# PEER gates by accumulating indirect DMAs into a table in device memory, in place of one-hot products on TensorE

## The chip, the core and the metric

The kernel runs on one core of one Trainium2 chip. The metric is the device time of one execution, in microseconds (us). The three timed executions of the kernel before took 2057.8, 2057.73 and 2062.33 us; their median is 2057.8 us. The engines are called by their names in the profile: PE is TensorE (PEld is its weight load), DVE is VectorE, ACT is ScalarE, POOL is GpSimd, and SP is SyncE, which here only issues DMAs.

## The reference, cut to what matters

One layer: a token mixer (projection with `w_in`, eight heads of stick-breaking attention, eight of retention, projection with `w_out`), a layer norm, the PEER block below, and a layer norm. There are 256 tokens of width 2048 and 16384 experts. Every token picks 16 experts for each of 8 heads; the pick's softmax weight is its gate:

```python
cand = (s_top[:, :, 0, :, None] + s_top[:, :, 1, None, :]).reshape(n_tok, PEER_HEADS, 256)
cand_idx = (i_top[:, :, 0, :, None] * PEER_KEYS + i_top[:, :, 1, None, :]).reshape(n_tok, PEER_HEADS, 256)
best, pos = lax.top_k(cand, PEER_TOPK)
expert_idx = jnp.take_along_axis(cand_idx, pos, axis=-1)
gate = jax.nn.softmax(best, axis=-1)
...
act = jax.nn.gelu(jnp.einsum('thkd,td->thk', u, xb), approximate=False)   # u = expert_u[idx]
return jnp.einsum('thk,thkd->td', g_b * act, v)                          # v = expert_v[idx]
```

## The kernel before, in words

The kernel gathers no expert rows. It computes the activation of every expert for every token, multiplies each by the sum of the gates that the token gave to that expert (zero where the token did not pick it), and multiplies the result with the whole of `expert_v`. The activations stand in SBUF in `wexp`: partition = expert within a tile, then `NT` = 128 tiles, then 256 tokens. Matrices are multiplied in float32r as three products of a high and a low part, so each piece of weights that SP loads into `raw` is split by ACT (`split_hi`) and by DVE or POOL (`split_lo`), and PE waits for both.

The stages in order of time:

- The projection with `w_in`: 14 column groups (`dense`), 16 k-tiles each. SP loads a group as 8 DMAs of 512 KB into the four slots of `raw`, and waits before each until the slot has been split (L279). The attention and retention heads are worked in between the k-tiles of groups 4 to 13. Then the projection with `w_out`, the layer norm and the query projection follow.
- The score stage: `PAIRS` = 64 pairs of expert tiles. Per pair, SP loads 2 MB of `expert_u` (L310), DVE transposes it (`turn_u`, L1393), ACT and POOL or DVE split it, PE multiplies it with the tokens (L640, L655), ACT and DVE bring the result out (`second_half_out`, `add_halves`), and ACT applies the gelu. In pairs 0 to 25 (`PAIRS_A`) the low parts are made by POOL (L1794), and DVE ranks the scores and decodes the picks (`rank_set`, `decode`). From pair 26 on DVE makes the low parts itself and POOL is free of them. The picks end in `pick_n`: for each token (partition), two key numbers and the gate of each of its 128 picks; `softmax_end` raises `topk_done`.
- The gates, in pairs 28 to 59: PE turns `pick_n` so that picks stand on partitions (`picks_after`, L670). For 4 tokens at a time (`GATES` = 64 groups, two in each pair) POOL subtracts an iota from the key numbers (`distances`), ACT turns the distances into one-hot rows (`hot_rows`, two activations), POOL multiplies one side by the gates (`weigh`), PE multiplies the two sides (`gates_after`, L682), and DVE multiplies the 4 tokens' columns of the whole of `wexp` by the result from PSUM (`apply_gates`, L1512). So that this can begin before all activations exist, POOL first fills the rows of `wexp` with ones (L1811, L1816, L1818), and the activations that come later go to a small buffer `late` and are multiplied in by POOL (`late_tile`, L1803).
- The value stage: 124 expert tiles in pairs, SP loading `expert_v` (L319), ACT and DVE splitting `wexp` (`split_w`) and the weights, PE accumulating in all eight banks (L404 to L406), then 4 held tiles, the residual, the layer norm and the stores.

The order on every engine is the order in which its block is written; the engines meet at semaphores only. Every DMA of this kernel is issued by SP.

Of the kernel before, what the change touches and what calls it, by code (L numbers as in the profile page):

```python
# [18 lines left out]
P = 128  # L19
# [29 lines left out]
PICKS = PAIRS_A  # L49
GATE0 = PICKS + 2  # L50
TABLE_PIECES, PIECE = 3, 1536
SB_AT = 4
# [3 lines left out]
GATES = SEQ // 4  # L56
LATE = 2 * PAIRS_A - 1
# [19 lines left out]
def layer_kernel(nc, x, w_in, sb_norm_w, ret_norm_w, w_out, ln1_w, ln1_b, w_pq, sub_keys,  # L77
# [4 lines left out]
    with ctx:  # L82
# [16 lines left out]
        picks_t = at("picks_t", [3, SEQ], f32, KEEP + 1024)  # L99
# [4 lines left out]
        hot = at("hot", [2, 2, 4, P], f32, KEEP + 5120)  # L104
        late = at("late", [2, SEQ], f32, KEEP + 13312)
        halves = at("halves", [4, SEQ], f32, KEEP + 9216)
        whalf_hi = at("whalf_hi", [2, SEQ], f32r, KEEP + 5120)
# [55 lines left out]

        ident, iota = small[:, 0, :], small[:, 1, :]
# [9 lines left out]
        def sem(name):  # L174
# [34 lines left out]
        picks_turned, picks_ready = sem("picks_turned"), sem("picks_ready")  # L209
        dist_ready, hot_ready, weighted, gate_ready, gates_free = (  # L210
            sem(n) for n in ("dist_ready", "hot_ready", "weighted", "gate_ready", "gates_free"))
        ranked, set_staged, set_kept = sem("ranked"), sem("set_staged"), sem("set_kept")
        ones_ready, late_used = sem("ones_ready"), sem("late_used")
        abs_ready, carried = sem("abs_ready"), sem("carried")
# [10 lines left out]
        MEAN, VAR, RSTD, NHALF, SHIFT, BN = 0, 16, 48, 80, 112, 160  # L225
# [47 lines left out]
        def _(sp):  # L273
# [9 lines left out]

            def out_pair(pair):
# [47 lines left out]
            sp.dma_start(norm_w[:, SBH * HD:D], ret_norm_w.partition_broadcast(P)).then_inc(norms_in, 16)  # L332
            with sp.Fori(SB_AT, 2 * SB_AT) as g:
# [57 lines left out]
        def _(pe):  # L391
# [242 lines left out]
            def score_pair(pair, after=None, parity=None):  # L634

                first = 0 if parity is None else 2 * parity
# [7 lines left out]
                for q in range(8):  # L644
                    t, end = q // 4, q % 4 == 3
                    if q % 4 == 0 and not (isinstance(pair, int) and pair < 2):
                        pe.wait_ge(score_free, pair * 2 + (t + 1 if parity is None else t - 1))
# [15 lines left out]
            def picks_after(q):  # L663

                if q == 5:
                    pe.wait_ge(topk_done, 1)
                    pe.wait_ge(score_free, 2 * PAIRS_A + 2)
# [28 lines left out]
            with pe.Fori(GATE0 + GATES // 2, PAIRS - 1) as i:  # L696
                score_pair(i)
# [1206 lines left out]
```

## Time and profile before

| | |
|---|---|
| median of the timed runs | 2057.8 us (2057.73 to 2062.33) |
| the profiled execution: device time | 2060.9 us |
| its span in the trace | 2059.1 us |
| mean granted clock of TensorE | 0.994 |
| PE busy | 2026.1 us (98%) |
| DVE busy | 1490.3 us (72%) |
| ACT busy | 1169.9 us (57%) |
| POOL busy | 601.4 us (29%) |
| DMA: moved, packets | 378.49 MB, 254250 |

Times in the views are microseconds from the start of the span. The busy share of an engine is a mean over stages that have different limits; the stages are told apart by their windows. Matmuls overlap each other, so that the sum of their durations is more than the time they take; the time of a piece of PE's work is read from the starts of two instructions.

### The profile page before, as it was taken

Reading aid. Unit: us, or ns where it says so; the run is one execution under the profiler, and the core shown is the slowest. Engines: PE = TensorE matmul, PEld = TensorE weight load, DVE = VectorE, ACT = ScalarE, POOL = GpSimd, SP = SyncE. Lnnn points to the kernel's source line nnn. Section 1 sums busy time; section 2 is a strip of 40 time slices with the busy share of each in tenths; the row PEclk is TensorE's granted clock in tenths of the full one; section 3 lists DMA queues with packets and bytes.
Section 4 is the critical chain, followed back from the end, with each engine's and each line's share of the span. In section 5 each row is a group of like instructions: output and inputs, shape, how many; then the busy total and the mean of one; then the engine's idle time right before and its main releaser. Section 6 shows DMA issues by size and latency. Waiting matters only on the chain.

```text
span 2059.1 us, 38813 instructions
## 1 busy us (share of the span) xinstructions
PE 2026.1 (98%) x10278; PEld 1717.0 (83%) x10278; DVE 1490.3 (72%) x2448; ACT 1169.9 (57%) x2084; POOL 601.4 (29%) x461
## 2 busy tenths in 40 slices
PE   8999999999999999999999999999999999999997
PEld 6888888777888888888888888888888888888886
DVE  4555776666589989999999999965555555555557
ACT  4455555444455555577777777555555555555553
POOL 0000330100099999965555555100000000000001
PEclk9999999999999999999999999999999999999999
DMA  7765554666596657665555555658756566565564
GB/s 242 230 177 167 172 168 138 218 191 180 160 210 187 189 160 186 178 172 164 161 162 161 162 162 162 181 194 229 217 192 192 193 193 193 193 194 193 192 193 146
DMA packets 254250, 378.49 MB, mean 184 GB/s; under 512 B 41856, under 2 KB 173056, under 8 KB 253568
## 3 DMA queue, kind: packets, MB, share of 16 engines
q1 hardware_dynamic: 254208, 377.98, 61.5%
q8 instruction: 20, 0.33, 0.1%
q14 instruction: 22, 0.18, 0.0%
HBM read 373.69 MB, written 4.19 MB: 184 GB/s over the span
## 4 chain that ended last, share of the span: by engine, by line
PE 82%; POOL 10%; issue 4%; DVE 2%; DMA 1%; ACT 1%; SPq 0%; POOLq 0%; ACTq 0%; DVEq 0%
PE ps L404 18%; PE ps L406 18%; PE ps L405 18%; PE ps L640 14%; POOL split_lo L1794 10%; PE ps L655 7%; PE ps L682 3%; PE ps L399 1%; DMA raw<-in_w_out 0%; DVE split_lo L1116 0%; DMA raw<-in_expert_v 0%; DMA x_nat<-in_x 0%; DVE end_lo L1660 0%; DVE stats L1670 0%; PE ps L614 0%
## 5 line engine op out<-in xcount | busy, mean ns | idle before, releaser
L1116 DVE TENSOR_TENSOR split_lo<-raw,split_hi 128x512 fp32r<-128x512 f32 x840 | 603.9, 722 | 491.1 <-ACT split_hi L759 489.9
L759 ACT ACTIVATE split_hi<-raw 128x512 fp32r<-128x512 f32 x840 | 528.8, 631 | 562.4 <-PE ps L406 545.9
L640 PE MATMUL ps<-act_both,split_hi 128*128 128x512 f32 x2048 | 564.2, 397 | 0.5 <-ACT split_hi L915 0.5
L640 PEld LDWEIGHTS ps<-act_both,split_hi 128*128 128x128 f32 x2048 | 350.3, 189 | 46.3 <-ACT split_hi L915 0.8
L404 PE MATMUL ps<-split_hi,whalf_hi 128*128 128x512 f32 x992 | 386.2, 389 | 0.0
L405 PE MATMUL ps<-split_lo,whalf_hi 128*128 128x512 f32 x992 | 386.0, 389 | 0.0
L406 PE MATMUL ps<-split_hi,whalf_lo 128*128 128x512 f32 x992 | 385.9, 389 | 0.0
L655 PEld LDWEIGHTS ps<-act_both,split_lo 128*128 128x128 f32 x2048 | 311.2, 188 | 49.6 <-POOL split_lo L1794 7.1
L655 PE MATMUL ps<-act_both,split_lo 128*128 128x256 f32 x2048 | 326.2, 281 | 0.6 <-POOL split_lo L1794 0.2
L1794 POOL TENSOR_TENSOR split_lo<-u_cols,split_hi 128x512 fp32r<-128x512 f32 x208 | 281.4, 1369 | 120.2 <-ACT split_hi L915 107.5
L404 PE MATMUL ps<-split_hi,act_both 128*128 128x512 f32 x688 | 276.0, 401 | 6.4 <-DVE split_lo L1116 6.2
L406 PE MATMUL ps<-split_hi,act_both 128*128 128x512 f32 x688 | 270.1, 393 | 0.0
L405 PE MATMUL ps<-split_lo,act_both 128*128 128x512 f32 x688 | 269.6, 392 | 0.0
L915 ACT ACTIVATE split_hi<-ps 128x512 fp32r<-128x512 f32 x304 | 177.0, 594 | 134.0 <-PE ps L655 97.4
L1781 POOL TENSOR_TENSOR stats<-stats 128x1 f32<-128x1 f32 (+1 forms) x6 | 9.7, 1610 | 833.6 <-DVE stats L1676 691.5
L1379 DVE TENSOR_TENSOR split_lo<-ps,split_hi 128x512 fp32r<-128x512 f32 x304 | 205.8, 681 | 30.1 <-ACT split_hi L915 30.0
L404 PEld LDWEIGHTS ps<-split_hi,whalf_hi 128*128 128x128 f32 x992 | 186.2, 188 | 39.3 <-DVE split_lo L1116 0.7
L406 PEld LDWEIGHTS ps<-split_hi,whalf_lo 128*128 128x128 f32 x992 | 186.2, 188 | 38.7
L405 PEld LDWEIGHTS ps<-split_lo,whalf_hi 128*128 128x128 f32 x992 | 186.2, 188 | 38.6
L915 ACT ACTIVATE split_hi<-u_cols 128x512 fp32r<-128x512 f32 x208 | 130.6, 631 | 124.0 <-PE ps L655 87.5
L1393 DVE STREAM_TRANSPOSE ps<-raw 128x1024 f32<-128x1024 f32 x152 | 191.3, 1259 | 5.8
L404 PEld LDWEIGHTS ps<-split_hi,act_both 128*128 128x128 f32 x688 | 130.4, 190 | 33.4 <-DVE split_lo L1116 5.6
(190 smaller groups left out, 1915.9 us busy)
## 6 DMA issues: line engine op xcount, KB each, us to landing
raw<-in_expert_u SPq DMA_DIRECT2D x1024, 128.0 KB, 2.9
raw<-in_expert_v SPq DMA_DIRECT2D x256, 512.0 KB, 4.6
raw<-in_w_in SPq DMA_DIRECT2D x112, 512.0 KB, 3.8
raw<-in_w_out SPq DMA_DIRECT2D x32, 512.0 KB, 4.5
raw<-in_w_pq SPq DMA_DIRECT2D x128, 128.0 KB, 2.8
cst<-in_tables SPq DMA_DIRECT2D x3, 768.0 KB, 4.8
x_nat<-in_x SPq DMA_DIRECT2D x4, 512.0 KB, 7.1
x_dram<-x_cols SPq DMA_DIRECT2D x1, 2048.0 KB, 8.3
```

Source lines behind the costliest of these rows:

```text
L404: nc.tensor.matmul(acc, l_hi, r_hi, start=first, stop=False)
L405: nc.tensor.matmul(acc, l_hi, r_lo, start=False, stop=False)
L406: return nc.tensor.matmul(acc, l_lo, r_hi, start=False, stop=last)
L640: return nc.tensor.matmul(ps[:, bank, :], split_hi[:, q % SPLITS, i * P:(i + 1) * P], act_both[:, k, :, :].rearrange("p a t -> p (a t)"), ...
L655: last = nc.tensor.matmul(ps[:, first + t, 0:SEQ], split_lo[:, q % SPLITS, i * P:(i + 1) * P], act_hi[:, k, :], start=False, stop=False)
L682: last = nc.tensor.matmul(ps[:, 2 + parity, i * P:(i + 1) * P], hot[:, parity, 1, i, :], hot[:, parity, 0, i, :], start=True, stop=True)
L759: nc.scalar.activation(split_hi[:, q % SPLITS, :], raw[:, q // 2, q % 2, :], ACT.Copy).then_inc(hi_ready, 1)
L915: nc.scalar.activation(split_hi[:, q % SPLITS, :], src, ACT.Copy).then_inc(hi_ready, 1)
L1116: vec.tensor_tensor(split_lo[:, q % SPLITS, :], raw[:, q // 2, q % 2, :], split_hi[:, q % SPLITS, :].bitcast(f32), ALU.subtract).then_inc( ...
L1379: vec.tensor_tensor(split_lo[:, q % SPLITS, :], ps[:, 4 + q % 4, :], split_hi[:, q % SPLITS, :].bitcast(f32), ALU.subtract).then_inc(lo_re ...
L1393: vec.transpose(dst.rearrange("p a (c g i) -> p g (a c) i", g=4, i=32), raw[:, k, :, :].rearrange("p a (b c q) -> p (a b) c q", b=2, c=8)) ...
L1794: eng.tensor_tensor(split_lo[:, q % SPLITS, :], u_cols[:, q // 2, q % 2, :], split_hi[:, q % SPLITS, :].bitcast(f32), ALU.subtract).then_i ...
```

## The change: what it does

A table `gate_dram` of 128 x 128 x 256 floats (partition, expert tile, token) is added in device memory, 16.8 MB. While the projection with `w_in` runs, SP fills it with zeros by 32 DMAs of 512 KB, five after each of the groups 4 to 7 and two after each of the groups 8 to 13 (`clear_gates`). DVE computes a place in the table for each pick (`places_out`: expert number times 256 and so on, plus the token's number, which `softmax_start` makes from `ident` and `iota`). POOL then issues 256 indirect DMAs: each adds one gate of each of 128 tokens to 128 places of the table. The 16 picks of one head and one half of the tokens have distinct places; between heads a place may repeat, so the next head of a half waits until the half's earlier DMAs have landed. When all have landed, POOL loads the table for one pair of tiles at a time (256 KB, two slots) and multiplies the pair's activations with it. All that served the one-hot products, the ones in `wexp` and the buffer `late` is gone; all 64 pairs go through the same code on PE, ACT and DVE, with four banks for scores in turn. ACT's `split_w`, the first step of the value stage, waits for POOL's product of the pair (`applied`).

```diff
+        gate_dram = nc.dram_tensor("gate_dram", (P * NT * SEQ, 1), f32, kind="Internal").ap()
+        gate_tiles = gate_dram.rearrange("(p n t) a -> p n (t a)", p=P, n=NT)
...
@@ sync @@
+            def clear_gates(n):
+
+                sp.dma_start(gate_tiles[:, bass.ds(n * 4, 4), :], zeros[:, :, :]).then_inc(zeroed, 16)
...
             with sp.Fori(SB_AT, 2 * SB_AT) as g:
                 dense(w_in_v, 0, g, True, g * (2 * COLS) - 7 * COLS)
+                for n in range(5):
+                    clear_gates(g * 5 + (n - 5 * SB_AT))
             with sp.Fori(2 * SB_AT, G_IN) as g:
                 dense(w_in_v, 0, g, True)
+                clear_gates(g * 2 + (ZEROS - 2 * G_IN))
+                clear_gates(g * 2 + (ZEROS + 1 - 2 * G_IN))
...
@@ tensor @@
-                        for i in range(4):
-                            last = nc.tensor.matmul(ps[:, 2 + parity, i * P:(i + 1) * P], hot[:, parity, 1, i, :],
-                                                    hot[:, parity, 0, i, :], start=True, stop=True)
-                        last.then_inc(gate_ready, 1)
...
-            with pe.Fori(1, PAIRS_A // 2) as i:
+            with pe.Fori(1, PAIRS // 2) as i:
                 for s in range(2):
                     score_pair(i * 2 + s, parity=s)
-            score_pair(PICKS, picks_after, parity=0)
-            score_pair(PICKS + 1)
-            with pe.Fori(GATE0, GATE0 + GATES // 2) as i:
-                score_pair(i, gates_after(i * 2 - 2 * GATE0))
...
@@ scalar @@
-            def hot_rows(n, parity):
...
             def split_w(n, t, static=False):
 
+                act.wait_ge(applied, (n // 8 + t // 2 + 1) if isinstance(n, int) else n // 8 + (t // 2 + 1))
...
@@ vector @@
-                vec.tensor_tensor(part, part, ps[:, 2 + parity, :].rearrange("p (t j) -> p j t", t=4), ALU.mult
-                                  ).then_inc(gates_free, 1)
...
             def softmax_start():
 
                 dve.wait_ge(set_kept, SOFT + 2)
+                chain.step(vec.tensor_tensor(rest[:, 0:P], ident, iota, ALU.mult))
+                chain.step(vec.tensor_reduce(stats[:, TOKEN:TOKEN + 1], rest[:, 0:P], AX.X, ALU.add))
+                chain.step(vec.tensor_scalar(stats[:, TOKEN + 1:TOKEN + 2], stats[:, TOKEN:TOKEN + 1], float(P), None, ALU.add))
...
+            def places_out():
+
+                for b in range(TB):
+                    chain.step(vec.scalar_tensor_tensor(
+                        out=pick_n[:, 0, b, :], in0=pick_n[:, 0, b, :], scalar=float(SEQ),
+                        in1=stats[:, TOKEN + b:TOKEN + b + 1].to_broadcast([P, P]), op0=ALU.mult, op1=ALU.add))
+                chain.step(vec.scalar_tensor_tensor(out=pick_n[:, 1, :, :], in0=pick_n[:, 1, :, :], scalar=float(NT * SEQ),
+                                                    in1=pick_n[:, 0, :, :], op0=ALU.mult, op1=ALU.add))
+                vec.tensor_copy(places[:, :, :], pick_n[:, 1, :, :]).then_inc(topk_done, 1)
...
@@ gpsimd @@
+                    def scatter(h, b):
+
+                        for k in range(h * TOPK, (h + 1) * TOPK):
+                            eng.indirect_dma_start(gate_dram, bass.IndirectOffsetOnAxis(ap=places[:, b, k:k + 1], axis=0),
+                                                   pick_n[:, 2, b, k:k + 1], None, compute_op=ALU.add
+                                                   ).then_inc(scattered[b], 16)
+
+                    pool.wait_ge(topk_done, 2)
+                    pool.wait_ge(zeroed, 16 * ZEROS)
+                    for h in range(PH):
+                        for b in range(TB):
+                            if h:
+                                pool.wait_ge(scattered[b], 16 * TOPK * h)
+                            scatter(h, b)
+                    for b in range(TB):
+                        pool.wait_ge(scattered[b], 16 * TOPK * PH)
...
+                    def apply_gates(pair, slot, turn):
+
+                        pool.wait_ge(gate_in[slot], turn * 16 + 16)
+                        pool.wait_ge(gelu_done, pair * 2 + 2)
+                        rows = wexp[:, bass.ds(pair * 2, 2), :]
+                        eng.tensor_tensor(rows, rows, gates[slot][:, :, :], ALU.mult).then_inc(applied, 1)
+                        pool.wait_ge(applied, pair + 1)
+
+                    for slot in range(GATE_SLOTS):
+                        load_gates(slot, slot)
+                    with pool.Fori(0, PAIRS // GATE_SLOTS - 1) as i:
+                        for slot in range(GATE_SLOTS):
+                            apply_gates(i * GATE_SLOTS + slot, slot, i)
+                            load_gates(i * GATE_SLOTS + (slot + GATE_SLOTS), slot)
```

What PE does in the first half of a gated pair of the kernel before (one tile of the pair, four quarters of its weights; L682 is the gate product, REGISTER_ALU a register step):

```order
1810 L640 MATMUL ps<-act_both,split_hi 128x512 [waits hi_ready]
1811 L640 MATMUL ps<-act_both,split_hi 128x512 x3
1812 L655 MATMUL ps<-act_both,split_lo 128x256 [waits lo_ready]
1813 L655 MATMUL ps<-act_both,split_lo 128x256 x3
1814 L648 REGISTER_ALU
1815 L640 MATMUL ps<-act_both,split_hi 128x512 [waits hi_ready]
1816 L640 MATMUL ps<-act_both,split_hi 128x512 x3
1817 L655 MATMUL ps<-act_both,split_lo 128x256 [waits lo_ready]
1818 L655 MATMUL ps<-act_both,split_lo 128x256 x3
1819 L679 REGISTER_ALU
1820 L682 MATMUL ps<-hot 128x128 [waits gates_free,weighted]
1821 L682 MATMUL ps<-hot 128x128 x3
```

In the changed kernel the rows of L682 and their waits are gone from PE's stream, and so are the six transposes of L670; the L640 and L655 rows are as many as before.

What POOL does in the changed kernel from the end of its split work on (`places` holds the places, `gates_59` and `gates_60` are the two slots, L1748 is the scatter, L1764 the load, L1772 the product):

```order
57 L1748 DMA gate_dram<-pick_n,places 4194304x1 x256
58 L1764 DMA gates_59<-gate_dram 128x512
59 L1764 DMA gates_60<-gate_dram 128x512
60 L1777 UNCONDITIONAL_BRANCH
61 L1777 ISA
62 L1770 ISA
63 L1772 ISA
64 L1772 TENSOR_TENSOR wexp<-wexp,gates_59 128x512
65 L1773 REGISTER_ALU
66 L1764 ISA
67 L1764 DMA gates_59<-gate_dram 128x512
```

All 256 scatters stand ahead of the first product on POOL, and in the kernel before there was no DMA on POOL at all.

What DVE does in the changed kernel between the end of the decoding and pair 26 (L1534 is the last step of the softmax, L1541 to L1546 are `places_out`):

```order
482 L1534 TENSOR_TENSOR pick_n<-best,gsum 128x256 [waits v_chain]
483 L1541 SCALAR_TENSOR_TENSOR pick_n<-pick_n,stats 128x128
484 L1541 SCALAR_TENSOR_TENSOR pick_n<-pick_n,stats 128x128 [waits v_chain]
485 L1544 SCALAR_TENSOR_TENSOR pick_n<-pick_n 128x256 [waits v_chain]
486 L1546 CAST places<-pick_n 128x256 [waits v_chain]
487 L1357 TENSOR_TENSOR wexp<-ps,halves 128x256 [waits half_out]
488 L1357 TENSOR_TENSOR wexp<-ps,halves 128x256 [waits half_out,lo_ready]
```

Four instructions are new there, ahead of the two sums that were next before.

## Rows read from the trace of the kernel before

**Rows 1.** Windows by stage: busy us and instructions of each engine, clock, DMA share, GB/s.
```profile
577.00:768.00 191.00, 191.00 (x1092) 166.94 (x1090) 180.98 (x494) 113.79 (x267) 177.36 (x137) 1.00 0.72 189
768.00:870.00 102.00, 100.93 (x557) 83.40 (x556) 98.36 (x108) 55.45 (x107) 99.45 (x67) 1.00 0.67 176
...
890.00:1306.00 416.00, 416.00 (x2568) 371.36 (x2568) 383.91 (x515) 307.12 (x513) 228.83 (x191) 1.00 0.56 163
...
1352.00:2022.00 670.00, 670.00 (x2955) 554.34 (x2954) 382.73 (x618) 349.99 (x620) 0.29 (x1) 1.00 0.62 199
```
**Rows 2.** The chain that ended last, from the page, by engine.
```profile
PE 82%; POOL 10%; issue 4%; DVE 2%; DMA 1%; ACT 1%; SPq 0%; POOLq 0%; ACTq 0%; DVEq 0%
```
**Rows 3.** Timeline of PE: a gated pair, the transposes, pairs without gates, first value product.
```profile
875.63 0.82 PE L670 MATMUL ps<-small,pick_n 128*128 128x128 f32 x6
876.20 1.18 PE L640 MATMUL ps<-act_both,split_hi 128*128 128x512 f32 x4
...
893.10 1.05 PE L682 MATMUL ps<-hot 128*128 128x128 f32 x8
...
906.06 1.05 PE L682 MATMUL ps<-hot 128*128 128x128 f32 x8
...
1316.00 1.31 PE L640 MATMUL ps<-act_both,split_hi 128*128 128x512 f32 x5
...
1327.21 1.31 PE L640 MATMUL ps<-act_both,split_hi 128*128 128x512 f32 x5
...
1349.86 0.40 PE L404 MATMUL ps<-split_hi,whalf_hi 128*128 128x512 f32 x1
```
**Rows 4.** Windows of one pair without gates, as Rows 1.
```profile
1316.00:1327.20 11.20, 11.20 (x66) 9.79 (x65) 11.04 (x15) 5.95 (x12) 1.48 (x2) 1.00 0.73 198
```
**Rows 5.** Timeline of DVE at the decoding and at its end.
```profile
765.74 3.13 DVE L1556 TENSOR_TENSOR onehot<-pos_f,small 128x512 f32<-128x512 f32 x2 [0.27 <-DVE pos_f L1537]
...
860.86 0.86 DVE L1594 TENSOR_TENSOR pick_n<-best,gsum 128x256 f32<-128x256 f32 x1
861.64 0.41 DVE L1405 TENSOR_TENSOR wexp<-ps,halves 128x256 f32<-128x256 f32 x1
865.41 0.42 DVE L1405 TENSOR_TENSOR wexp<-ps,halves 128x256 f32<-128x256 f32 x1 [3.36 <-POOL split_lo L1794]
```
**Rows 6.** Groups by line and form: busy, mean ns of one, idle before.
```profile
L1836 POOL TENSOR_TENSOR hot<-hot,picks_t 128x512 f32<-128x512 f32 x64 | 66.7, 1042 | 173.0 <-ACT hot L945 173.0
...
L1781 POOL TENSOR_TENSOR stats<-stats 128x1 f32<-128x1 f32 x4 | 3.2, 791 | 781.3 <-DVE stats L1676 691.5 <-DVE stats L1320 89.8
...
L1537 DVE CAST pos_f<-pos_i 128x512 f32<-128x512 uint32 x1 | 1.4, 1406 | 0.0
```
**Rows 7.** SP's DMA issues by source line: duration ns min/median/max.
```profile
L310 SPq DMA_DIRECT2D raw<-in_expert_u x1024: 311/317/1622, 549.4 to 1331.9; - x171
L377 SPq DMA_DIRECT2D x_back<-x_dram x16: 382/593/3099, 1412.0 to 1441.4; - x16
```
**Rows 8.** DMA issues: KB each, median us to landing.
```profile
raw<-in_expert_u SPq DMA_DIRECT2D x1024, 128.0 KB, 2.9
...
small<-in_small_tables SPq DMA_DIRECT2D x1, 128.0 KB, 2.1
```
**Rows 9.** Windows in the value stage and the projection, as Rows 1.
```profile
1411.00:1443.00 32.00, 32.00 (x141) 26.13 (x141) 17.94 (x30) 15.96 (x29) 0.00 (x0) 1.00 0.88 215
...
1475.00:1507.00 32.00, 32.00 (x143) 26.51 (x142) 18.65 (x30) 16.39 (x29) 0.00 (x0) 1.00 0.60 193
...
90.00:100.00 10.00, 10.00 (x45) 8.26 (x45) 5.34 (x8) 4.42 (x7) 0.00 (x0) 1.00 0.84 279
...
128.00:151.30 23.30, 23.30 (x112) 19.34 (x111) 14.08 (x22) 13.04 (x23) 1.04 (x1) 1.00 0.59 171
```

More of the change, by code:

```diff
@@ L103, in layer_kernel @@
         pick_n = at("pick_n", [3, TB, P], f32, KEEP + 5120)
-        hot = at("hot", [2, 2, 4, P], f32, KEEP + 5120)
-        late = at("late", [2, SEQ], f32, KEEP + 13312)
+        gates = [at(f"gates{i}", [2, SEQ], f32, KEEP + (13312, 2048)[i]) for i in range(GATE_SLOTS)]
         halves = at("halves", [4, SEQ], f32, KEEP + 9216)
+        zeros = at("zeros", [4, SEQ], f32, KEEP + 9216)
         whalf_hi = at("whalf_hi", [2, SEQ], f32r, KEEP + 5120)
@@ L631, in rest_of_scores, with score_pair @@
                         score(j)
-            def score_pair(pair, after=None, parity=None):
-                first = 0 if parity is None else 2 * parity
+            def score_pair(pair, after=None, parity=0):
+                first = 2 * parity
                 def wide(bank, q, i):
@@ L963, in keep_set, with u_pair @@
                                      ACT.Copy).then_inc(set_kept, 1)
-            def u_pair(pair, part_a, next_a, parity=None, is_late=False, groups=None, kept=None, staged_set=None, after=None):
+            def u_pair(pair, part_a, next_a, parity, kept=None, staged_set=None, after=None):
                 for q in range(4, 8):
@@ L982, in u_pair @@
                     stage_set(*staged_set)
-                split_u(pair + 1, 0, next_a)
-                if groups is not None:
-                    hot_rows(groups, 0)
-                for q in range(1, 4):
+                for q in range(4):
                     split_u(pair + 1, q, next_a)
-                    if q == 2 and is_late:
-                        gelu(pair, 0, True)
-                    elif q == 2 and not (isinstance(pair, int) and pair == 0):
-                        gelu(pair, -1, False)
+                    if q == 2 and not (isinstance(pair, int) and pair == 0):
+                        gelu(pair, -1)
                 second_half_out(pair, 1, parity)
-                if groups is not None:
-                    hot_rows(groups + 1, 1)
             act.wait_ge(x1_out, 16)
+            act.wait_ge(zeroed, 16 * ZEROS)
             act.sem_inc(set_kept, 2)
@@ L1046, in _ @@
             u_pair(PAIRS_A - 1, True, False, 1)
[L1047 to L1051 removed]
+            with act.Fori(PAIRS_A // 2, PAIRS // 2 - 1) as i:
+                for s in range(2):
+                    u_pair(i * 2 + s, False, False, s)
+            u_pair(PAIRS - 2, False, False, 0)
             for q in range(4, 8):
@@ new lines, in _, with load_gates @@
+                    pool.wait_ge(topk_done, 2)
[7 more added lines that the diff above has]
+                        pool.wait_ge(scattered[b], 16 * TOPK * PH)
+                    def load_gates(pair, slot):
+                        eng.dma_start(gates[slot][:, :, :], gate_tiles[:, bass.ds(pair * 2, 2), :]
+                                      ).then_inc(gate_in[slot], 16)
```

220 lines of the change are left out of this document (56 added, 164 removed).

## The prediction, made before the changed kernel had run

> **What bounds the kernel now.** I read the page's chain first: 82% of the span is PE and 10% POOL's split [rows 2]. Then I cut the span into stages [rows 1]. In the gated part of the score stage (890 to 1306 us) and in the value stage (1352 to 2022) PE is busy in every microsecond at full clock; DVE is at 92% in the first of them and at 57% in the second. In the decoding (768 to 870) PE loses only 1 us, but DVE (98.36 of 102) and POOL (99.45) are full, and POOL's share of the chain is there and before. So time is gained by whatever leaves PE's stream after 870 us, as long as nothing else then comes late, and DVE's extra work costs in the decoding and hardly anywhere else.
>
> **What is removed from PE.** The reader compares starts in PE's timeline [rows 3]. A pair with gates takes 906.06 - 893.10 = 12.96 us; a pair without takes 1327.21 - 1316.00 = 11.21 us. The difference, 1.75 us, is eight matmuls of one-hot rows (16 records). There are 32 gated pairs: 32 x 1.75 = 56.0 us. The six transposes of the picks hold PE for 876.20 - 875.63 = 0.57 us. Together 56.6 us off PE. That pairs really run at 11.21 us without gates is seen in [rows 4]: DVE is busy 11.04 of 11.20 us and still keeps up. The changed pair has the same 8 splits, 4 transposes and 2 sums on DVE, fewer activations on ACT, and on POOL something that reads no activations; so I take 11.21 for all 38 pairs from pair 26 on. ACT's one-hot rows, POOL's distances and DVE's 64 products into `wexp` all lay beside PE and bring nothing by themselves. The memsets of ones lay on POOL beside PE too: nothing.
>
> **What is added on DVE.** Three small instructions at the start of the softmax stand where DVE is full. The smallest rows near them: 0.4 us for a 128x256 sum, 0.86 for one that reads SBUF twice [rows 5]. I take 1 us in all for a 128x128 product, a reduction and one addition of a column; bounds 0 (if PE's lead swallows it) and 2.6 (three times 0.86). `places_out` has two instructions on 128x128, one on 128x256 and a cast of 128x256: at most 0.86 for each of the first three and half of the 1.41 us cast of 128x512 [rows 6], 3.3 us, likelier 2. Behind them on DVE stand two sums, and the second waited 3.36 us for POOL anyway [rows 5]; the new work fits into that wait. Cost 0; without that cover it would be 2 us, once. The copies of the turned picks (three, 0.4 us each) leave DVE in pair 26, also hidden.
>
> **What is added in the projection.** SP puts zeros behind the loads in its own queue: five DMAs of 512 KB after each of groups 4 to 7. A group takes 23.3 us and moves its 4.2 MB at a DMA share of 0.59, 171 GB/s [rows 9]. That is 290 GB/s at a full share; the burst at 90 to 100 us (two weights of the norms, 1 MB, in front of the loads) ran at 279 GB/s with a share of 0.84 and PE lost nothing. With zeros a group of this kind moves 6.8 MB in 23.3 us, 292 GB/s: close to all there is. The queue is in order, so the next load stands behind 2.6 MB, about 2.6 / 0.279 = 9.4 us, and lands some 9.4 + 1.9 (its own 512 KB) + 2 (a short landing) = 13 us after the last load of the group was issued. At that time about 4 slots of `raw` are full or on the way, 8 k-tiles of 1.46 us (23.3 / 16) = 11.6 us, and up to 4 split k-tiles, 5.8 us, stand between them and PE. So ACT starves for 1 to 2 us and PE should just not. I take 3 us over the four groups; bounds 0 and 4 x 3 = 12 us (if writes run no faster than 200 GB/s: 13.1 us of zeros, then 17 against 11.6 + 2 to 3 that the split tiles still cover after ACT's and DVE's own time). Groups 8 to 13 carry 5.2 MB in 23 us, 228 GB/s, which is hidden, as the value stage's own 215 to 233 is.
>
> **The scatters, on which everything hangs.** POOL may start when the places are ready: 861.6 in DVE's timeline plus about 2, plus 4 for the two costs above, so at 867 us. The value stage begins on PE at 1349.86 before [rows 3], so at 1349.9 - 56.6 + 4 = 1297 now. ACT's first `split_w` waits for the first product, and behind it on ACT stand all splits of `expert_v`, so PE would stand still. Ahead of PE's first matmul go a load (2.9 us to landing [rows 8]), POOL's product of 128x512 (1.04 [rows 6]), two splits of the weights and of `wexp` on ACT and DVE (about 2.5): 6 to 7 us. The last scatter must therefore have landed by 1290. That leaves 1290 - 867 = 423 us for 256 of them, **1.65 us each**. Beyond it each 0.1 us more costs 25.6 us.
>
> No row shows a DMA issued by POOL, nor an accumulating one. From below: SP's issues take 0.32 us for 128 KB of `expert_u` and 0.59 us (median) for 1024 pieces of 128 bytes [rows 7]; then 256 x 0.59 = 151 us, all hidden. From above: the shortest landing in the trace, 2.1 us [rows 8], if POOL or the DMA were held until the data is there: 256 x 2.1 = 538 us, 115 too many. Between: POOL's smallest instruction takes 0.79 us [rows 6]; with an issue like SP's on top, 0.79 + 0.32 to 0.59 = 1.1 to 1.4. I take 1.3 us, 333 us in all, done at about 1200 with 90 us to spare. It is nearer to the break-even than I like.
>
> The Trainium skill ("DMA: Bandwidth & Descriptors", Specifications) gives about 1 us to the first byte for a DMA issued from GpSimd and 0.6 for one from SP. By it 256 x 1 = 256 us would be an estimate of the issuing, and it would be hidden. The same page (Anatomy of one DMA) fits 2.0 us of fixed time to every such DMA and gives most of it to the write's receipt; held one after another, 512 us would be 89 us too many. Which of the two holds POOL, no run of before shows; the rivals below carry it.
>
> On the DMA engines: each scatter gives each of 16 engines 8 single floats, 2048 in all per engine. The small pieces of the trace are those of `x_back`: 16 DMAs x 1024 pieces fall into 1411 to 1443 us. That window moved 6.9 MB, 4.8 of them `expert_v`; at the later window's 0.60 for 193 GB/s these take 0.46 of the share, so 0.42 x 16 x 32 = 215 us of engine time went to 16384 pieces, 13 ns each [rows 9]. At 13 ns the scatters take 27 us of each engine. The upper bound is again the shortest landing, 2.1 us for an engine's 8, 0.26 us each, 538 us. An addition must read before it writes; I take 0.1 us, 205 us in all, beside loads that use 0.62 of a share, so tight but not late. Between a head's 16 scatters and the wait for them stand the 16 of the other half, some 20 us, against a landing of 2 to 3: those waits cost nothing.
>
> **The products and table loads.** Once the scatters are done, POOL's round for a pair is a load issue (about 1), a landing (2.9, with the other slot's work beside it) and 1.04 of product: some 3 us per pair, against 10.9 us that PE takes for a pair of value tiles (670 us for about 61.5 pairs [rows 1]). It gains 8 us on every pair; the 16.8 MB of table loads add 25 GB/s to 199. Cost 0.
>
> **The sum.** 2060.9 (profiled execution) - 56.6 + 1 + 3 = 2008.3. The profiled execution lay 3.1 us above the median of the timed runs, so I forecast **2005 us** for the median, with 1998 to 2015 as this case's own range (0 and 2.6 for the softmax, 0 to 12 for the zeros).
>
> **The rivals.**
> - *The scatters issue too slowly.* POOL is held longer than 1.65 us by each. For it: the two shortest landings of the trace are above 2 us, and an indirect DMA needs 128 addresses worked out. Against it: no DMA of this trace holds its issuer for its landing. Time: 2005 + 256 x (c - 1.65); at c = 2.1, 2120 us, slower than before; at 1.75, 2031, still faster. It turns at c = 1.86. PE would show one gap ahead of the first L404.
> - *The DMA engines drain the additions too slowly.* A float read from and written to device memory holds an engine for more than 0.2 us, so that the waits between heads bite. For it: nothing of this kind is in the trace and the engines are 0.56 to 0.73 busy. Against it: 13 ns for small pieces. At the upper bound 2048 x 0.26 = 538 us, again 2120 us. The Trainium skill ("DMA: Bandwidth & Descriptors", Two DMAs through the same engine are not ordered) tells that a second read-modify-write close behind the first read stale data, and none did with five or more packets between; so several overlap, which speaks for the lower figure. No run of before shows it.
> - *The zeros stall the projection* by 12 us and not 3: 2014 us, still faster.
> - That the change leaves the matmuls in is excluded by PE's order of instructions.
>
> **How the numbers follow.** Forecast 0.44. Zeros stall more 0.07. Slow issue 0.35, of which 0.09 is still faster (c below 1.83), 0.03 the same and 0.23 slower. Slow draining 0.14, of which 0.13 slower and 0.01 the same. A difference under 0.3% (6 us) can't be told from none. Faster 0.44 + 0.07 + 0.09 = 0.60, same 0.04, slower 0.36. The range: 1998 below; above, 2125 takes in both rivals at their bound and leaves some 0.15 for worse.
>
> **What would show it.** Right: L640's starts 11.21 us apart per pair from 870 on, no L682, and the first L404 at about 1297; POOL's 256 issues end before 1290; PE busy 100% from 580 to 1960. The zeros: ACT's L759 waiting for `raw` in groups 5 to 8, PE not. Wrong: a gap of PE before the first L404, with POOL's stream full of L1748 up to it (slow issue) or full of waits for `scattered` at every 16th (slow draining); or pairs slower than 11.21 us while the scatters run, which would be `expert_u` arriving late or DVE disturbed.

## The result, and the profile after

The changed kernel takes 2079.7 us (median of 4 runs, 2075.8 to 2081.2) against 2060.1 us for the kernel before in the same runs (2057.7 to 2062.4). The ratio is 1.0097, with a 95% interval of 1.0084 to 1.0109: it is slower by about 1%, and the forecast of 2005 us was wrong in its sign. Three views of the kernel after tell most of it. First its page: PE's granted clock, DMA and GB/s in 40 equal slices, the engines in the chain, the scatters' group (busy us, mean ns, idle us before them), and the software queue.

```profile
PEclk9999999999999999999999999599999999999999
...
GB/s 253 227 275 273 206 214 177 222 163 205 162 208 189 187 156 182 180 193 188 187 188 187 189 187 148 10 270 259 281 272 219 194 192 193 192 194 193 194 193 135
...
q0 software_dynamic: 41984, 16.93, 7.3%
...
PE 55%; POOL 29%; issue 8%; DVE 3%; DMA 2%; SPq 1%; ACT 1%; POOLq 0%; ACTq 0%; DVEq 0%
...
L1748 POOL DMA_INDIRECT gate_dram<-pick_n,places x256 | 398.5, 1557 | 81.2 <-issue 80.3
```

POOL has gone from 10% to 29% of the chain [rows 2], and in the 26th slice (1299 to 1351 us) next to nothing is moved (10 GB/s) and TensorE has its lower clock (5 tenths, 1.2 GHz). The source line of the scatters, with the shortest, median and longest duration in ns, and what it waited for:

```profile
L1748 POOL DMA_INDIRECT gate_dram<-pick_n,places x256: 1552/1556/1812, 865.2 to 1342.5; - x128
its engine sat idle before it (us, times) until:
  issue: 80.3, 255
  DVE places L1546: 0.9, 1
```

A scatter holds POOL for 1.56 us and 0.30 us pass before the next, 1.86 us each; over all, (1342.5 - 865.2) / 255 = 1.87. Not one wait for an earlier scatter is among them; all 255 are "issue". What happens at the end of them is in the timeline of all engines (start, duration, in brackets the idle time before and its releaser):

```profile
1342.46 1.55 POOL L1748 DMA_INDIRECT gate_dram<-pick_n,places  x1 [0.30 <-issue]
1346.28 1.20 POOL L1764 DMA_DIRECT2D gates<-gate_dram  x2 [2.27 <-DMA gate_dram<-pick_n,places]
1349.63 1.26 POOL L1772 TENSOR_TENSOR wexp<-wexp,gates 128x512 f32 x1 [2.15 <-DMA gates<-gate_dram]
1350.92 0.42 ACT L1017 ACTIVATE whalf_hi<-wexp 128x256 fp32r<-128x256 f32 x1 [63.51 <-POOL wexp L1772]
...
1354.15 0.77 PE L417 MATMUL ps<-split_hi,whalf_hi 128*128 128x512 f32 x1 [62.10 <-DVE split_lo L1072]
```

PE had finished the scores at 1292.0 us, 58 us before the old start of the value stage, 1349.86 [rows 3]. It then stood for 62.1 us. So the first value matmul comes 4.3 us later than before. The value stage, from there to the end of the span, takes 2078.1 - 1354.15 = 723.9 us against 2059.1 - 1349.86 = 709.2. The two parts, +4.3 and +14.7, are the 19.0 us between the spans. To place the 14.7 us I count matmuls in windows that start at the first value matmul (PE alone: window, busy, clock, DMA share, GB/s). Before:

```profile
1349.86:1355.86 6.00, 6.00 (x28) 1.00 0.51 173
1355.86:1399.86 44.00, 44.00 (x196) 1.00 0.72 240
1399.86:1459.86 60.00, 60.00 (x264) 1.00 0.81 227
1459.86:1509.86 50.00, 50.00 (x222) 1.00 0.61 195
```

And after:

```profile
1354.15:1360.15 6.00, 6.00 (x18) 0.66 0.67 223
1360.15:1404.15 44.00, 44.00 (x196) 1.00 0.85 296
1404.15:1464.15 60.00, 53.25 (x221) 0.94 0.89 256
1464.15:1514.15 50.00, 49.99 (x220) 1.00 0.81 278
```

A matmul goes every 0.227 us at full clock. Ten are missing in the first 6 us, where the mean clock is 0.66 (2.3 us), and 43 in the window of 60 us (9.8 us); from 1564 on the counts agree to one. The remaining 2 to 3 us are in the tail: from the last product with `whalf_hi` (L404 before, L417 after) to the end of the span it is 34.8 us before (2024.3 to 2059.1) and 37.8 after (2040.3 to 2078.1). The runs below have 33.8 to 39.0 there, and nothing explains the spread. In the long window ACT waited for weights (timeline of ACT):

```profile
1435.53 1.15 ACT L740 ACTIVATE split_hi<-raw 128x512 fp32r<-128x512 f32 x2 [7.52 <-DMA raw<-in_expert_v]
...
1462.75 2.39 ACT L740 ACTIVATE split_hi<-raw 128x512 fp32r<-128x512 f32 x4 [4.93 <-DMA raw<-in_expert_v]
```

Three things can be behind that: POOL's loads of the table, which after the scatters come every 3.6 us ((1573.8 - 1346.3) / 63); POOL's products beside DVE's splits (L1072: 885 ns each from 1360 to 1580 us, 694 later); or `x_back`, 16 DMAs of small pieces that SP issues just then, 1418.6 to 1456.5 us (1412.0 to 1441.4 before [rows 7]).

### The profile page after: what moved, and what is told of

Read it like the earlier page. It is cut to its first block, busy times and chain, and to the rows that moved or that the text cites. A ratio compares the mean times of both kernels' runs of the same rounds, so it can differ in the third digit from the quotient of the medians.

```text
span 2078.1 us, 37602 instructions
## 1 busy us (share of the span) xinstructions
PE 1971.8 (95%) x9760; PEld 1659.4 (80%) x9760; DVE 1488.0 (72%) x2388; ACT 1054.7 (51%) x1956; POOL 868.5 (42%) x638
## 4 chain that ended last, share of the span: by engine, by line
PE 55%; POOL 29%; issue 8%; DVE 3%; DMA 2%; SPq 1%; ACT 1%; POOLq 0%; ACTq 0%; DVEq 0%
POOL gate_dram L1748 19%; PE ps L417 18%; PE ps L419 17%; PE ps L418 17%; POOL split_lo L1735 10%; SPq L390 1%; DMA raw<-in_expert_v 1%; DVE split_lo L1072 1%; DMA raw<-in_w_out 0%; ACT split_hi L740 0%; PE ps L412 0%; DMA x_nat<-in_x 0%; DVE end_lo L1600 0%; DVE stats L1610 0%; DMA raw<-in_w_pq 0%
## 5 line engine op out<-in xcount | busy, mean ns | idle before, releaser
L1072 DVE TENSOR_TENSOR split_lo<-raw,split_hi 128x512 fp32r<-128x512 f32 x840 | 634.8, 760 | 464.6 <-ACT split_hi L740 463.3
L417 PE MATMUL ps<-split_hi,whalf_hi 128*128 128x512 f32 x992 | 388.3, 391 | 68.9 <-DVE split_lo L1072 68.9
L1748 POOL DMA_INDIRECT gate_dram<-pick_n,places x256 | 398.5, 1557 | 81.2 <-issue 80.3
L668 PEld LDWEIGHTS ps<-act_both,split_lo 128*128 128x128 f32 x2048 | 311.4, 188 | 51.3 <-POOL split_lo L1735 9.3
L668 PE MATMUL ps<-act_both,split_lo 128*128 128x256 f32 x2048 | 327.1, 282 | 1.1 <-POOL split_lo L1735 0.8
L896 ACT ACTIVATE split_hi<-ps 128x512 fp32r<-128x512 f32 x304 | 182.0, 599 | 199.6 <-PE ps L668 94.2
L417 PE MATMUL ps<-split_hi,act_both 128*128 128x512 f32 x688 | 275.5, 400 | 6.8 <-DVE split_lo L1072 6.5
L417 PEld LDWEIGHTS ps<-split_hi,whalf_hi 128*128 128x128 f32 x992 | 187.4, 189 | 109.1 <-issue 62.4
```

The source lines that it names most:

```text
L417: nc.tensor.matmul(acc, l_hi, r_hi, start=first, stop=False)
L668: last = nc.tensor.matmul(ps[:, first + t, 0:SEQ], split_lo[:, q % SPLITS, i * P:(i + 1) * P], act_hi[:, k, :], start=False, stop=False)
L896: nc.scalar.activation(split_hi[:, q % SPLITS, :], src, ACT.Copy).then_inc(hi_ready, 1)
L1072: vec.tensor_tensor(split_lo[:, q % SPLITS, :], raw[:, q // 2, q % 2, :], split_hi[:, q % SPLITS, :].bitcast(f32), ALU.subtract).then_inc( ...
L1748: eng.indirect_dma_start(gate_dram, bass.IndirectOffsetOnAxis(ap=places[:, b, k:k + 1], axis=0), pick_n[:, 2, b, k:k + 1], None, compute_o ...
```

## The experiments

Theory A: POOL's own time for an adding scatter, 1.86 us, sets the gap. Rivals: the scatters drain slowly (B), or something else in the change costs what PE gave up. For the value stage: C, the table loads crowd out `expert_v`; D, POOL's products slow DVE; G, which I formed later, `x_back` collides with them.

### No scatters, and one head fewer

```diff
-                    for h in range(PH):
+                    for h in range(7):      # e2; in e1 the loop and its waits are left out
...
-                        pool.wait_ge(scattered[b], 16 * TOPK * PH)
+                        pool.wait_ge(scattered[b], 16 * TOPK * 7)
```

> All 256 scatters are left out (the table stays zero, so the gates are missing from the output); zeros, table loads, products and waits stay. Theory (POOL's issuing of the scatters ends last): the gap of 62.1 us before the first value matmul goes, and the table loads now go out at the pace of the gelus in the score stage, so the 14.7 us that the value stage is longer than before go as well: 2079.7 - 62.1 - 14.7 = 2003 us, 0.97 of the kernel before. Rival (zeros, table loads or DVE's new work cost something themselves): 2010 us or more. Rival (DVE is slowed by POOL's product in the score stage, where it is 92% busy): score pairs longer than 11.21 us, 2010 us or more.

> The scatters of the eighth head are left out (its gates are missing from the output): 224 in place of 256. Theory (POOL's issuing, 1.864 us each): the first value matmul comes 865.2 + 224 x 1.864 + 11.8 = 1294.6 us into the span, against 1292.1 for the end of the scores, so the gap shrinks from 62 to about 2.5 us; the table loads still rush ahead in the value stage and cost some 12 us there: 2079.7 - 59.6 - 2 = 2018 us, still faster than before (0.98). Rival (the DMA engines' draining is what ends last, with POOL's rows only following): idle time before every 16th scatter, and a gap that is not shorter by 32 x 1.864.

Measured: 2010.1 us without scatters (ratio 0.9744, 0.9721 to 0.9767), 2018.0 us with seven heads (0.9785, 0.9766 to 0.9805). 32 scatters fewer give back 61.7 us, where 32 x 1.86 is 60, and the 224 others only 8 more. The duration of one is unchanged (source line of e2):

```profile
L1748 POOL DMA_INDIRECT gate_dram<-pick_n,places x224: 1552/1556/1813, 864.8 to 1281.8; - x112
```

Theory A stands: the cost is a threshold. Scatters hide behind the scores up to 1292 us, and each further one costs its full 1.86 us. The run without any also shows that the rest of the change is worth what the forecast of 2005 us said, to within 5 us. It missed its own expectation of 2003 by 7: the gap is gone, but its value stage, 713.6 us (2011.6 - 1298.05), is still 4.4 longer than before.

The run with seven heads shows something about the clock too. PE stood there for 4.4 us only, not for 62, and came back no faster:

```profile
1296.00:1302.00 6.00, 5.96 (x15) 0.53 0.69 220
```

15 matmuls in place of 28, at a granted clock of 0.53. In e7 below PE stood for 2.2 us, and 19 were done (0.72). Without a stop (e1) all 28 were. So the lower clock at the start of the stage is not the price of a long wait only: a stop of 2 to 4 us had it as well.

### What a scatter's time is made of

```diff
-  bass.IndirectOffsetOnAxis(ap=places[:, b, k:k + 1], axis=0), pick_n[:, 2, b, k:k + 1], None, compute_op=ALU.add
+  bass.IndirectOffsetOnAxis(ap=places[:, b, k:k + 1], axis=0), pick_n[:, 2, b, k:k + 1], None                      # e3
+  bass.IndirectOffsetOnAxis(ap=places[0:64, b, k:k + 1], axis=0), pick_n[0:64, 2, b, k:k + 1], None, compute_op=ALU.add  # e4
```

> The 256 scatters write instead of add (where two heads of a token picked the same expert one gate is lost). Theory A (POOL works out 128 addresses, whatever the DMA then does): still 1.56 + 0.30 us per scatter, 2080 us. Theory B (the addition makes the descriptors dearer, it needs a read of the target too): below 1.65 us per scatter, so that the gap goes: 2005 to 2020 us.

> Every scatter covers 64 of its 128 tokens (the gates of the others are missing from the output); still 256 scatters. Theory A (the time goes by the number of places): 0.30 + about half of 1.56 = 1.1 us each, done long before the scores, about 2003 us. Theory B (a fixed time per DMA): 1.86 us each and 2080 us. Between them the two parts can be read off.

With 64 places in place of 128 the kernel takes 2039.0 us (0.9891, 0.9865 to 0.9916). The sources of the scatters, e4 and then e3:

```profile
L1748 POOL DMA_INDIRECT gate_dram<-pick_n,places x256: 1402/1411/1661, 863.3 to 1303.5; - x128
```

```profile
L1748 POOL DMA_INDIRECT gate_dram<-pick_n,places x256: 954/958/1912, 863.8 to 1194.8; - x128
```

Half the places save 1556 - 1411 = 145 ns. If the time is linear in the places (two points can't show it), a place is 2.3 ns and the other 1.57 us (with the 0.30 between) are fixed. My figure of 1.1 us for e4 was wrong, but the kernel's time follows the measured one: 256 x 0.145 = 37 us, 40.7 measured. The addition is 0.60 us of POOL's 1.56; a plain scatter is 1.26 us with its gap, very near to the forecast's 1.3, and POOL was done at 1196 us. So theory B is right on the scatter. Yet the kernel with plain scatters took 2342.2 us (1.1361, 1.1323 to 1.1400), which neither theory expected. Windows of it, columns as [rows 1]:

```profile
880.00:940.00 60.00, 8.79 (x24) 6.64 (x24) 4.90 (x6) 2.07 (x4) 45.36 (x49) 0.53 0.11 27
940.00:1000.00 60.00, 8.78 (x24) 6.62 (x24) 3.66 (x5) 2.37 (x5) 45.67 (x48) 0.55 0.05 9
```

`expert_u` comes at 9 to 27 GB/s, with the DMA engines 5 to 11% busy. So it isn't bandwidth. SP's own instructions between 880 and 1195 us, first in e3, then in the kernel after:

```profile
L318 SPq MOVE raw<-in_expert_u x32: 4/695/723, 881.1 to 1162.2; - x32
L318 SPq DMA_DIRECT2D raw<-in_expert_u x32: 4/691/1409, 882.5 to 1163.0; - x32
```

```profile
L318 SPq DMA_DIRECT2D raw<-in_expert_u x453: 15/317/524, 879.9 to 1195.0; - x151
L318 SPq MOVE raw<-in_expert_u x452: 2/29/330, 880.4 to 1194.9; - x151
```

Even a MOVE of SP takes 695 ns in place of 29. Beside plain scatters of POOL SP's stream is slow; beside adding ones it is not. But that is not all that PE waits for. One round of e3 in the timeline, and ACT's wait over the whole stretch (880 to 1195 us):

```profile
947.71 0.60 ACT L896 ACTIVATE split_hi<-ps 128x512 fp32r<-128x512 f32 x1 [21.81 <-remote]
950.23 1.05 PE L668 MATMUL ps<-act_both,split_lo 128*128 128x256 f32 x4
970.10 0.60 ACT L896 ACTIVATE split_hi<-ps 128x512 fp32r<-128x512 f32 x1 [21.49 <-remote]
```

```profile
ACT split_hi L896 <- remote: 311.3, 15, 22.3
```

Nearly the whole 315 us are 15 such rounds of 22 us. In each, ACT's next split waits for `split_free`, which PE raises with the last matmul of a piece, here the last of the four L668. It had ended at 951.28, and ACT started 18.8 us later (16 to 20 in the rounds from 900 us on); in the kernel after the two are 0.5 to 0.8 us apart. So signals between engines are late as well, and with them everything. How much of it is SP's stream and how much the signals, and what plain scatters do to either, is not shown.

### The waits between heads

```diff
-                    for h in range(PH):
-                        for b in range(TB):
+                    for b in range(TB):
+                        for h in range(PH):        # e8; in e9 also without compute_op
```

> The kernel after with the two halves of the tokens scattered one after the other (all eight heads of the first half, then of the second) instead of by turns, so that each head's scatters must have landed before the next head's may be issued, with nothing of the other half between them. Theory A (POOL's issue of 256 scatters at 1.86 us each is the whole wait, and the landings are hidden by the turns): 14 waits for a landing of some 2.3 us, as the last one showed, come on top: the gap grows by 32 us to about 94 us, and the kernel takes about 2112 us. Rival B (the scatters of a head drain slowly behind the issue, and the turns merely cover it): each wait is as long as a head's drain, up to 30 us, which gives up to 2500 us. No change at all, 2080 us, would say that the issue itself already waits for the landing.

> Scatters that write instead of add (the sums over the heads are left out), and the halves one after the other, so that POOL waits for the landing of each head's 16 scatters before the next 16. It asks why expert_u came at 9 to 27 GB/s while plain scatters were issued. Theory E (the writes drain slowly, so that they stand ahead of the other loads): each of the 14 waits is 20 us or longer, and POOL ends the scatters after 1400 us. Rival F (the writes land as fast as the adding ones, 3.7 us after the last issue, and what stalls the loads is something else in their issue): POOL ends the scatters at about 866 + 256 x 1.26 + 14 x 3.4 = 1236 us, and the loads get their share back only then, or a little in each of the 14 waits; the kernel takes 2340 to 2390 us.

e8 takes 2132.2 us (1.0358, 1.0330 to 1.0386), 20 us more than expected. One of the 14 waits in POOL's timeline, and their sum in the scatters' source line:

```profile
894.49 1.55 POOL L1748 DMA_INDIRECT gate_dram<-pick_n,places  x1 [0.30 <-issue]
899.89 1.55 POOL L1748 DMA_INDIRECT gate_dram<-pick_n,places  x1 [3.84 <-DMA gate_dram<-pick_n,places]
```

```profile
  issue: 90.0, 241
  DMA gate_dram<-pick_n,places: 41.5, 14
```

The landing is exposed: 41.5 - 14 x 0.30 = 37.3 us, 3 us on average (waits of 1.7 to 3.9 us), where I had sized it by the single landing of 2.27 us at the end. The other 14 us of the 52 by which the first value matmul is later (1406.0 against 1354.15) are pauses of 1.8 to 4.3 us within a head: "issue" is 90.0 us for 241 times here, where the kernel after has 80.3 for 255. Why they come is open. A head's sixteen take no 30 us to drain, so B falls, and the turns of the two halves do hide every landing. In e9 (2332.8 us; 1.1335, 1.1286 to 1.1384; a little below the 2340 to 2390 of F) the plain ones land even sooner, and POOL is done at 1215 us (1236 expected):

```profile
891.27 0.96 POOL L1748 DMA_INDIRECT gate_dram<-pick_n,places  x1 [2.52 <-DMA gate_dram<-pick_n,places]
```

So writes that drain slowly (E) are not what holds the kernel up. Through what the engines meet is left open.

### Where the value stage lost 14.7 us

Pacing: a load of the table only after ACT has rounded an earlier pair (e5, and e7 with seven heads). No loads: the products are kept and the gates of most pairs are not loaded (e6, where the products also wait only for the first load of their slot).

```diff
+                            pool.wait_ge(w_hi, i * 4 + (2 * slot + 4 - 12))                      # e5, e7: i from 3 on
                             load_gates(i * GATE_SLOTS + (slot + GATE_SLOTS), slot)              # left out in e6
```

> The kernel after, with one edit: from the ninth pair on POOL issues the next table load only after ACT has rounded the weighted activation of an earlier pair, so that the loads and products no longer run ahead of TensorE. The same work in all. The kernel after spent 14.7 us more in the value stage than the one before (723.9 against 709.2 us from the first value matmul to the end). Theory C (POOL's 256 KB table loads, one per 3.5 us after the scatters, crowd out the loads of expert_v): the value stage shrinks by about 12 us, the kernel takes about 2067 us, and the waits of ACT for raw expert_v in the stage go. Rival D (VectorE is slowed by POOL's products, or it is the clock after the idle stretch): no or little change, 2075 to 2080 us. The wait for the scatters of some 62 us stays under both.

> The kernel after with only the first two table loads kept, and all the products: from the third pair on the products use the gates of the first two pairs (the weights of the others are left out). POOL's products then run as fast as they can, with no DMA of the table beside them. Theory C (the table loads crowd out expert_v): the value stage goes from 723.9 to about 711 us and the kernel takes about 2067 us. Rival D (POOL's products beside VectorE's splits): the stage stays near 724 us or longer, 2080 us. If both this one and the paced one stay at 2080, it is the clock after the idle stretch.

> Seven of the eight heads scattered (the gates of the last head are left out) and the loads of the table paced as in the run above. With seven heads alone the kernel took 2018.0 us, with the wait for the scatters down to some 6 us. Theory C: the value stage gives back what the rush cost there too, 2006 to 2010 us. Rival D: 2017 to 2018 us.

Measured: e5 2075.5 us (1.0085, 1.0071 to 1.0099), e6 2078.7 us (1.0100, 1.0085 to 1.0116), e7 2013.6 us (0.9774, 0.9759 to 0.9789). All three intervals overlap those of the kernels they are compared with (the kernel after for e5 and e6, e2 for e7), so a gain from pacing is not clear of noise; the medians say 4 us, not the 12 of C. PE's windows of e5 and of e6 at the place where the kernel after lost 43 matmuls:

```profile
1404.90:1464.90 60.00, 56.51 (x241) 0.97 0.85 243
```

```profile
1400.10:1460.10 60.00, 57.09 (x228) 0.97 0.73 201
```

With paced loads 23 of 264 are still missing. With no loads at all and products back to back, DVE is the one that is full (all engines, columns as [rows 1]):

```profile
1360.00:1410.00 50.00, 49.69 (x200) 35.87 (x199) 50.00 (x43) 23.56 (x41) 39.34 (x26) 1.00 0.65 218
```

DVE is busy 50.00 of 50 us and does 43 instructions, where the kernel before did 46 in 28.68 us. D is thus a real effect: the Trainium skill ("SBUF — State Buffer", SBUF: two separate sides) says that a DVE instruction with two SBUF inputs and a GpSimd instruction that reads SBUF lock each other out of a shared pair of ports, each for its whole length. The trace agrees: a split takes up to 1785 ns here and 694 alone. But it binds only in e6, with products closer together than the table's loads let them come. And the run without scatters, which has no load or product in this stage, also lost 16 matmuls in the window with `x_back` (248 of 264). That left G:

```diff
+            v_pairs(5, 41)
             for b in range(TB):
-                v_pairs(5 + 2 * b, 7 + 2 * b)
+                v_pairs(41 + 2 * b, 43 + 2 * b)
...
-            v_pairs(5 + 2 * TB, HELD_AT // 2)
+            v_pairs(41 + 2 * TB, HELD_AT // 2)
```

> The kernel after, with SP's 16 DMAs of x_back (small pieces, needed only at the end) moved from behind the sixth and eighth pair of expert_v to behind pairs 42 and 44. In the kernel after they fall at 1418 to 1457 us, into the time in which POOL loads a tile of the table every 3.5 us, and there ACT waited 7.5 us and 4.9 us for expert_v. Theory G (x_back and the table loads together are what PE loses 10 us to between 1404 and 1464): the value stage goes from 723.9 to about 716 us and the kernel takes about 2071 us. Theory C alone (table loads, with x_back innocent) or D (POOL's products beside VectorE): 2077 to 2080 us.

> Both edits: x_back late and the table loads paced. Theory G: of the 14.7 us that the value stage gained, only the half-clock restart is left (2 to 3 us), so a stage of about 712 us and a kernel of 2067 us. If C and G are two names for one collision, it is no better than the late x_back alone, 2071 us. Theory D: 2075 us as the paced one had.

> No scatters (the gates are left out) and x_back late. Without scatters the kernel took 2010.1 us with 713.6 us in the value stage, 4.4 more than the kernel before, and lost 16 matmuls in the minute of x_back. Theory G: these come back, 709 to 710 us in the stage and 2006 us in all. Otherwise 2010 us.

Measured: e10 2072.0 us (1.0064, 1.0050 to 1.0079), e11 2074.9 us (1.0082, 1.0068 to 1.0096), e12 2005.8 us (0.9740, 0.9724 to 0.9756). PE's windows of e10, with the unpaced rush of POOL still in them:

```profile
1354.42:1360.42 6.00, 6.00 (x19) 0.68 0.70 225
1360.42:1404.42 44.00, 44.00 (x196) 1.00 0.87 292
1404.42:1464.42 60.00, 60.00 (x267) 1.00 0.86 291
...
1754.42:2004.42 250.00, 248.41 (x1097) 1.00 0.65 200
```

All 43 matmuls are back, at 291 GB/s and with DVE's splits at 940 ns on average. So the table loads and the products cost PE nothing by themselves; `x_back` on top of them did. The interval of e10 lies clear of the kernel after's. Only the restart is left (19 against 28), and `x_back` takes 8 matmuls at its new place (1097 against 1105). Part of the 43 is `x_back` alone: it took 16 in e1 and 20 in e12 with nothing of POOL's beside it, where the kernel before lost 3 (264, where e10 and e12 have 267 without `x_back`). Why it costs more in the changed kernels is open.

Pacing on top (e11) brings nothing more. G said 2067 and got 2075; `x_back` late costs 18 matmuls there, 10 more than in e10, which is 2.3 of the 8 us. The intervals of e10 and e11 overlap and both profiled executions have a span of 2070.8 us, so these two aren't told apart; that of e11 overlaps the kernel after's too. e12 has the 2005.8 us that G forecast, but it doesn't show G: against the kernel before in the same runs its ratio is that of e1 (0.9740 and 0.9744), and its stage stayed at 713.6 us (the 16 came back, 20 were lost at the new place). That its profiled execution had the first value matmul 5.5 us earlier than e1's is 1.8 us from ahead of the scores (they start at 568.4 and 566.6) and 3.6 us from pairs 26 to 39, where DVE waited for `expert_u` in e1.

## Why the prediction was wrong, step by step

- *PE is relieved by 56.6 us*: right. From the first matmul of pair 26 to the last of the scores it is 425.6 us in place of 482.4, 56.8 less; pairs under the scatters take 11.21 us each. PE was ready 58 us earlier, because the score stage also began 2.5 us sooner (565.8 against 568.3); in the runs with the zeros it begins anywhere between 563.3 and 568.4.
- *Softmax and places, +1 us and a hidden 2 us*: `places_out` took 4.4 us (860.46 to 864.9), 1.35 us for each 128x128 step where I had bounded it by 0.86 [rows 5]. That cost nothing: the first scatter was at 865.2, 867 forecast. Pairs 0 to 25 take 300.2 us against 298.9, 1.3 for the 1 of the softmax.
- *Zeros, +3 us (0 to 12)*: 0. The four groups ran at 269 to 289 GB/s with PE busy in all of their 93 us, and 443 matmuls done where the kernel before did 441. First of the four windows, columns as [rows 9]:

```profile
100.00:123.00 23.00, 23.00 (x107) 18.99 (x107) 13.42 (x20) 13.79 (x22) 1.04 (x1) 1.00 0.83 289
```

- ***1.3 us per scatter*: the step that failed.** It was 1.86, 0.21 above the break-even of 1.65. I had put POOL's smallest instruction and SP's issue together (0.79 + 0.32 to 0.59, rounded up to 1.3), which by luck fits a plain scatter (1.26). That the addition costs the issuing engine 0.60 us more stood in no row. The rival "the scatters issue too slowly" is what happened, and its formula gives 2005 + 256 x 0.21 = 2059 us. By the prediction's own working that is the point (c = 1.86) where its gain is just used up; the 1% of loss is the rest. The 21 us from there to the measured time are the value stage (14.7), the next item (3) and the 2.3 us by which the kernel before, too, ran slower in these runs (2060.1) than in those shown (2057.8).
- *From the last scatter to PE, 2.3 + 6 to 7 us*: 10.1 us (1344.0 to 1354.15). My formula counted 7 us from the end of the issue and left the landing out, 3.1 us too little. The scatters began 1.8 us earlier than it said, and 1.87 in place of 1.86 for each adds 2.6; together some 3 us more, to rounding.
- *Products and table loads, cost 0*: 14.7 us. By themselves they cost nothing (e10), but the rush after the late scatters met `x_back` (9.8), and the value stage began at the lower clock (2.3); the prediction had neither. The cover that I named, 8 us gained on each pair, was never looked at for what else is in SP's queue in those first 100 us.
- *The DMA engines' time per small addition, 0.1 us*: about half. While the scatters run, the share is 0.95 at 191 GB/s (900 to 911.2 us) against 0.73 at 198 in [rows 4]: 0.22 x 16 x 11.2 = 39 us for 6 x 128 additions, an estimate of 0.05 us each. The rival of slow draining is refuted (no wait between heads in the kernel after; e8).

On the issuing time, the Trainium skill ("DMA: Bandwidth & Descriptors", Specifications) gives about 1 us to the first byte for a DMA from GpSimd. It is a latency, and taken as an issue rate it would have given 256 us; the trace shows 477. The same page (Anatomy of one DMA) gives 2.0 us of fixed time per DMA, most of it the write's receipt. The landings are near it, 1.7 to 3.9 us of POOL's wait after the last of sixteen, and they don't hold POOL in between: it stands only where the program waits (e8). The bounds of the prediction (0.59 to 2.1) were honest and held 1.86; the sign hung on the point taken between them, 1.3, and no row priced an addition.

## What to carry to other kernels

Work that is hidden behind a stage costs nothing up to a threshold and its full price beyond it. Work out the threshold per item first (here 1.65 us for each of 256), and see on which side of it the bounds of the item lie; where they straddle it, the forecast is a bet on one number. Count an indirect DMA by the time that it holds POOL, more than by its bytes (1.41 us for 64 places, 1.56 for 128). When a late stage is released, its producers run in a burst: look at which other transfers sit in that window, since moving 16 unrelated DMAs brought 7.7 of the 19.6 us back. No version with all gates beat the kernel before. By the runs each us that POOL is done sooner gives back one, so POOL would have to be some 20 us shorter to draw level (12 with `x_back` late) and some 60 to bring the forecast time. The runs that are faster (e1, e2, e4, e7, e12) leave gates out.

## What the runs showed of the hardware

- An indirect DMA that adds holds POOL for 1.56 us for 128 places of 4 bytes and 1.41 us for 64; a plain one 0.96 us. Another 0.30 us pass before the next. POOL's load of 256 KB takes it 0.55 us.
- Sixteen adding scatters have landed 1.7 to 3.9 us after the last was issued (e8; 2.3 at the end of the kernel after, 4.9 in e2); plain ones after 1.4 to 2.5 (e9).
- While plain scatters to device memory are issued (e3), SP's instructions take 0.69 us in place of 0.03 (MOVE) and of 0.32 (DMA); in e9 a MOVE takes 0.69 and a DMA 0.32. In e3 ACT starts 16 to 20 us after PE's last matmul, whose signal it waits for, in place of 0.5 to 0.8. With adding scatters neither changes.
- After 62 us of idle, TensorE's granted clock was near the lower level (1.2 GHz): matmuls took 0.63 us and not 0.39 for some 4 us, and 9 to 12 of them were lost. After 4.4 us of idle it was 13 (e2), after 2.2 us 9 (e7), after none 0 (e1).
- DVE's split of 128x512 took 694 ns alone, and 812 to 940 ns on average from 1360 to 1580 us, beside POOL's products (the kernel after, e10, e11).
